# Expert gate and up products by Strassen's method, on two 128x64 column tiles

## The reference, cut to what matters

```python
def expert_choice_ffn(h, router, e_gate, e_up, e_down):
    ...
    cap = EC_FACTOR * t // N_EXPERTS
    ...
    gate, idx = lax.top_k(jnp.swapaxes(aff, 1, 2), cap)
    ...
    xe = h[bidx, idx]
    hid = jax.nn.silu(jnp.einsum('becd,edf->becf', xe, e_gate)) * jnp.einsum('becd,edf->becf', xe, e_up)
    ye = jnp.einsum('becf,efd->becd', hid, e_down) * gate[..., None].astype(h.dtype)
    return jnp.zeros_like(h).at[bidx, idx].add(ye)
```

## Time and profile before

| what | value |
|---|---|
| time, median of 3 runs | 3619.27 us (3618.79 to 3622.28) |
| span of the profiled execution | 3612.2 us |
| time of the runs outside the span (the difference of the two) | 7.1 us |
| TensorE matmul busy | 3408.1 us, 94% of the span |
| TensorE weight loads busy | 2976.7 us, 82% |
| VectorE busy | 1102.5 us, 31% |
| ScalarE busy | 735.5 us, 20% |

### The profile page before, as it was taken

The page is one execution under the profiler, slowest core; times in us unless marked ns, Lnnn a source line. Parts: engine busy times, 40 slices in busy tenths (PEclk is TensorE's granted clock), DMA queues, the critical chain, the costliest instruction groups (busy, mean ns, idle before and its releaser), DMA issues.

```text
span 3612.2 us, 83473 instructions
## 1 busy us (share of the span) xinstructions
PE 3408.1 (94%) x37698; PEld 2976.7 (82%) x37698; DVE 1102.5 (31%) x2770; ACT 735.5 (20%) x1815; POOL 385.0 (11%) x536
## 2 busy tenths in 40 slices
PE   7989898898999997499999999999999999999998
PEld 3575767667455544499999999999999999999998
DVE  4566666575344444411111111111111111111113
ACT  3435344343244433000000000000000000000002
POOL 0141514233211000000000000000000100000001
PEclk9999999999999998799999999999999999999999
DMA  8200000000311122697777778787778878777775
GB/s 353 71 5 9 18 10 17 5 20 5 102 32 26 43 77 93 226 362 264 281 269 275 268 274 275 264 288 258 272 276 280 275 267 283 263 281 269 274 264 185
DMA packets 500080, 666.46 MB, mean 185 GB/s; under 512 B 31598, under 2 KB 438406, under 8 KB 496654
## 3 DMA queue, kind: packets, MB, share of 16 engines
q1 hardware_dynamic: 494030, 641.74, 50.5%
q0 software_dynamic: 5520, 19.34, 2.0%
q10 hardware_dynamic: 176, 0.05, 0.0%
HBM read 631.68 MB, written 28.30 MB: 183 GB/s over the span
## 4 chain that ended last, share of the span: by engine, by line
PE 58%; SPq 1%; DMA 0%; DVE 0%; ACT 0%; issue 0%; DVEq 0%
PE banks L2465 38%; PE banks L2477 19%; PE banks L2488 0%; PE banks L2423 0%; DMA e_wd<-in_e_down 0%; SPq L2335 0%; SPq L2339 0%; SPq L2336 0%; SPq L2334 0%; ACT e_wd L2558 0%; PE banks L2447 0%; DVE e_ye L2632 0%; DVE e_wu L2718 0%; DVE e_wu L2661 0%; DVE e_xe L2707 0%
## 5 line engine op out<-in xcount | busy, mean ns | idle before, releaser
L2465 PE MATMUL banks<-e_xT,e_wg 128*128 128x144 f32 x5632 | 747.9, 287 | 1.9 <-DVE e_xT L2598 1.6
L2477 PE MATMUL banks<-e_hid,e_wd 128*128 128x144 f32 x5632 | 748.1, 287 | 0.0
L2465 PE MATMUL banks<-e_xT,e_wu 128*128 128x144 f32 x5632 | 747.6, 287 | 0.0
L2465 PEld LDWEIGHTS banks<-e_xT,e_wg 128*128 128x128 f32 x5632 | 713.8, 191 | 2.4 <-DMA e_wd<-in_e_down 2.3
L2465 PEld LDWEIGHTS banks<-e_xT,e_wu 128*128 128x128 f32 x5632 | 713.8, 191 | 0.0
L2477 PEld LDWEIGHTS banks<-e_hid,e_wd 128*128 128x128 f32 x5632 | 711.1, 191 | 0.0
L2608 DVE TENSOR_TENSOR e_tm<-banks,e_sg 128x144 f32<-128x144 f32 x352 | 108.3, 308 | 1790.3 <-ACT e_sg L2544 1790.3
L2544 ACT ACTIVATE e_sg<-banks 128x144 f32<-128x144 f32 x352 | 102.1, 290 | 1937.6 <-PE banks L2465 1937.6
L606 PE MATMUL banks<-hT_x,wblk 128*128 128x512 f32 (+1 forms) x624 | 212.7, 496 | 0.0
L606 PEld LDWEIGHTS banks<-hT_x,wblk 128*128 128x128 f32 x624 | 102.8, 192 | 100.1 <-issue 98.5
L1398 DVE TENSOR_TENSOR r_TW<-r_TW,banks 128x256 f32<-128x256 f32 (+1 forms) x360 | 129.3, 392 | 78.3 <-PE banks L830 74.1
(11 more groups left out here) (383 smaller groups left out, 3572.0 us busy)
## 6 DMA issues: line engine op xcount, KB each, us to landing
e_wg<-in_e_gate SPq DMA_DIRECT2D x176, 1024.0 KB, 5.2
e_wu<-in_e_up SPq DMA_DIRECT2D x176, 1024.0 KB, 7.5
e_wd<-in_e_down SPq DMA_DIRECT2D x176, 1024.0 KB, 10.2
h_wmod<-in_w_mod SPq DMA_DIRECT2D x24, 1024.0 KB, 15.2
wblk<-in_w_in SPq DMA_DIRECT2D x22, 512.0 KB, 21.5
h_x<-in_x_sample SPq DMA_DIRECT2D x8, 512.0 KB, 6.8
wo<-in_w_out SPq DMA_DIRECT2D x2, 2048.0 KB, 12.0
scratch_ffn<-hT_x SPq DMA_DIRECT2D x8, 512.0 KB, 5.2
```

The source lines that it names most:

```text
L2465: last = nc.tensor.matmul(bank[6 + b % 2][:, j * TOK:(j + 1) * TOK], w[s][:, k, f], xT[e % 2][:, k, :], start=(k == 0), stop=(k == KD - 1))
L2477: last = nc.tensor.matmul(bank[k // PER_BANK][:, c:c + TOK], wd[s][:, b % DUO, k * P:(k + 1) * P], hid[:, b % 2, :], start=(b == 0 and k % ...
```

## The change

Gate and up products of a duo are no longer made block by block as 8 pieces of 128 inputs each, but for the whole duo at once as a 2x2 block product: the weights of a duo are cut into halves by input (pieces 0 to 3 and 4 to 7) and by feature (block 0 and block 1), the tokens into halves by input and by token (72 and 72). Where a plain 2x2 block product takes eight half-size products, Strassen's method in Winograd's form takes seven, of which four use sums of blocks as an operand, and the four results are sums of the seven. So:

- VectorE forms three weight sums and one in place per duo, for gate and up together, 1024 elements per partition each (`sums_begin`, `sums_middle`, `sums_end`), two duos ahead, and four token sums per expert (`token_sums`).
- TensorE makes seven products for gate and seven for up, each over four pieces of 128 inputs, with 72 moving columns. The products of gate stand in bank 6 and those of up in bank 7. There is one set of banks, so gate and up of duo n+1 wait until those of n have been mixed (`gu_ok`).
- After them, ScalarE copies the first product out (`first`), and VectorE adds the results together in four steps (`mix`), then multiplies as before, for the whole duo at once (`gated`, `hidden`, 288 elements).
- Every matmul of the stage's main loop loads 128x64 weights and writes 64 PSUM partitions. Two neighbours write the two halves. The transposes of the loop become products with the identity matrix, in the same two halves (`turned`).
- Gate and up weights go into one buffer `wgu`, four deep, that is free when gate and up of the duo four earlier are done; down weights stay six deep. TensorE's order is gate and up of n+1, then the two halves of down of n, with transposes behind the halves in groups of four.

The diff, cut to its core:

```diff
-        wg = [sb(f"wg{i}", [P, KD, DUO * P]) for i in range(DEPTH)]
-        wu = [sb(f"wu{i}", [P, KD, DUO * P]) for i in range(DEPTH)]
-        wd = [sb(f"wd{i}", [P, DUO, D]) for i in range(DEPTH)]
+        wgu = [sb(f"wgu{i}", [P, 2, KD, DUO * P]) for i in range(WG)]
+        wd = [sb(f"wd{i}", [P, DUO, D]) for i in range(WD)]
+        wsum = [sb(f"wsum{i}", [P, 3, 2, HALF, P]) for i in range(2)]
...
+                    if n >= WG:
+                        sp.wait_ge(gu_ps, n - WG + 1)
+                    sp.dma_start(wgu[n % WG][:, 0, :, :], gv[:, e, :, f]).then_inc(g_in[n % WG], 16)
+                    sp.dma_start(wgu[n % WG][:, 1, :, :], uv[:, e, :, f]).then_inc(g_in[n % WG], 16)
+                    if n >= WD:
+                        sp.wait_ge(used, n - WD + 1)
...
+                def turned(b, out, src, n=P):
+
+                    for c in CS:
+                        if c.start < n:
+                            c = slice(c.start, min(c.stop, n))
+                            last = nc.tensor.matmul(bank[b][c, out], src[:, c], K.ident[:, :], start=True, stop=True)
+                    return last
...
+                def gate_up(n):
...
+                    pe.wait_ge(g_in[s], 32 * (n // WG + 1))
+                    pe.wait_ge(wsum_ok, n + 1)
+                    if n:
+                        pe.wait_ge(gu_ok, n)
...
+                    for g in range(2):
+                        w = wgu[s][:, g, :, :]
+                        products = ((w[:, k1, f1], x[:, k1, t1]), (w[:, k2, f1], x[:, k2, t1]),
+                                    (ws[:, 1, g, :, :], xs[:, 1, :, :]), (w[:, k1, f2], xs[:, 0, :, :]),
+                                    (ws[:, 0, g, :, :], x[:, k1, t2]), (ws[:, 2, g, :, :], x[:, k2, t2]),
+                                    (w[:, k2, f2], xs[:, 2, :, :]))
+                        for q, (a, b) in enumerate(products):
+                            for k in range(HALF):
+                                for c in CS:
+                                    last = nc.tensor.matmul(bank[6 + g][c, q * HT:(q + 1) * HT], a[:, k, c], b[:, k, :],
+                                                            start=(k == 0), stop=(k == HALF - 1))
+                    last.then_inc(gu_ps, 1)
...
+                gate_up(0)
+                for n in range(N):
+                    if n + 1 < N:
+                        gate_up(n + 1)
+                    down(n, 0)
+                    between(*divmod(n, ND), 0)
+                    down(n, 1)
+                    between(*divmod(n, ND), 1)
...
+                def sums_begin(n):
+
+                    a11, a12, a21, a22 = weight_blocks(n)
+                    dve.wait_ge(g_in[n % WG], 32 * (n // WG + 1))
+                    V.tensor_tensor(wsum[n % 2][:, 0, :, :, :], a11, a21, ALU.subtract).then_inc(ws_ok, 1)
+                    V.tensor_tensor(a21, a21, a22, ALU.add).then_inc(ws_ok, 1)
...
+                def mix(n):
...
+                    dve.wait_ge(gu_ps, n + 1)
+                    dve.wait_ge(first_ok, n + 1)
...
+                    V.tensor_tensor(gu[:, :, 0:4:3, :], first[:, :, :].unsqueeze(2).broadcast_to([P, 2, 2, HT]),
+                                    blocks(1, 2), ALU.add).then_inc(mix_ok, 1)
+                    dve.wait_ge(mix_ok, 2 * n + 1)
+                    V.tensor_tensor(mixed[:, :, :, :], gu[:, :, 3:4, :].broadcast_to([P, 2, 2, HT]), blocks(3, 2), ALU.add)\
+                     .then_inc(mix_ok, 1)
+                    dve.wait_ge(mix_ok, 2 * n + 2)
+                    V.tensor_tensor(gu[:, :, 1:3, :], mixed[:, :, :, :], blocks(5, 2), ALU.add)
+                    V.tensor_tensor(gu[:, :, 3:4, :], mixed[:, :, 1:2, :], blocks(3, 1), ALU.add).then_inc(gu_ok, 1)
...
+                for n in range(N):
+                    e, j = divmod(n, ND)
+                    mix(n)
+                    if n + 2 < N:
+                        sums_begin(n + 2)
+                    gated(n)
+                    if n + 2 < N:
+                        sums_middle(n + 2)
+                    hidden(n)
+                    if n + 2 < N:
+                        sums_end(n + 2)
```

319 lines of the change are left out of this document (167 added, 152 removed).

## The result

| | before | after |
|---|---|---|
| time, median | 3620.18 us (3618.79 to 3622.28, 4 runs) | 3724.38 us (3716.04 to 3726.98, 4 runs) |
| ratio, 95% interval | | 1.0289 (1.0275 to 1.0302) |
| span of the profiled execution | 3612.2 us | 3714.3 us |

The changed kernel is slower by 2.9% where the forecast had it faster by 2.9%. The page after, its lines that answer to the earlier trace rows: the span and the busy times, TensorE and VectorE in 40 slices, the transfers of instructions, the chain that ended last, and four groups of TensorE with their idle time and what ended it.

The account below looks back on a forecast made before the run. TensorE's instructions, one after another, were taken to bound the expert stage. Span 3612.2 - 148 (gate and up) + 30 (transposes) + 12 (start) + 3 (end) = 3509 us, plus 7.1 outside: 3516 us, range 3500 to 3570.

Parts of the forecast that it names:

- Gate and up, the slots: Gate and up products, expert stage: two halves run side by side, 112 slots of 62.5 ns, 7.00 us, 0.84 us less per duo.
- A: Rival on gate and up: slots last 64.4 ns or a little more, 37 us more, 3553 us; chance 0.17.
- B: Rival on gate and up: the two halves take turns, slots of 109 to 112 ns, about 4440 us; chance 0.06.
- Down and transposes: Expert stage: down stays at 122.5 ns a slot, 3.92 us per duo; transposes in two halves cost 30 us more.
- VectorE: VectorE's sums, mixing and multiplications in the expert stage: 7.5 of 10.92 us per duo, staying below TensorE.
- C: Rival: VectorE becomes the bound, needing sums of over 2.0 us; at 2.3 us a sum, 3715 us; chance 0.05.
- D: Rival: the new wait for `mix` shows; ending 0.3 us after down adds 53 us, 3569 us; chance 0.08.
- Start and end: Expert stage's ends: first transposes and sums delay the start by 12 us, late mixing in the last expert costs 3 us.
- Transfers: Weight transfers in the expert stage: 288 GB/s needed, four buffers instead of six, refills issued 22 us ahead; hidden.
- starts hold TensorE: Rival on TensorE's instruction starts: over 34 ns each the change would lose; the trace shows 14.4 ns; chance 0.01.
- T1b: Experiments' theory, not the prediction's: instruction pieces wait while weight transfers run; without those, about 3550 us or less expected.
- T1a: Experiments' theory, not the prediction's: instruction pieces come late by their own latency; without weight transfers, 3700 to 3725 us expected.

## Why the prediction was wrong

**What bounds the kernel.** Right for the kernel before. "So the stage costs what TensorE's instructions cost one after another" is what did not carry over: it holds as long as the instructions are there.

**Gate and up, the slots.** Right: 62.5 ns, so A (64.4 ns) and B (halves in turns) did not happen. The choice of the line through the long forms was right too: 72, 96 and 144 columns lie on one line of 0.83 ns a column through 62.5, 82.4 and 122.0 ns. That line would give 56 ns at 64 columns, a little less than the 58 ns of the four-tile row. That this row is bound by its weight loads, the reason given, was not tested.

**Down and transposes.** Right: 3.9 us, and 30 us against 31.8 measured with tiles alone.

**VectorE.** Right in its parts: the sums took 1.22 us, 1.14 apart, the mix 0.45, 0.45, 0.45 and 0.30:

```profile
2508.33 0.45 DVE L2687 TENSOR_TENSOR e_gu<-e_first,banks 128x288 f32<-128x288 f32 x1 [4.92 <-PE banks L2495]
2508.82 0.45 DVE L2690 TENSOR_TENSOR e_mixed<-e_gu,banks 128x288 f32<-128x288 f32 x1
2509.30 0.45 DVE L2693 TENSOR_TENSOR e_gu<-e_mixed,banks 128x288 f32<-128x288 f32 x1
2509.68 0.30 DVE L2694 TENSOR_TENSOR e_gu<-e_mixed,banks 128x144 f32<-128x144 f32 x1
```

`mix` ends at 2509.98, and the next gate and up products start at 2512.43, behind down and some transposes: hidden, as forecast. C and D did not happen. The sign "VectorE at 65 to 70% in the stage" was missed (57.78 of 100 us), as a duo took longer; without weight transfers it is 66.08.

**Start and end.** Right: 12 us and 3 us were forecast. Products began at 1503.91 against 1494.90, with 2.22 us between duo 0 and 1, and down of the last duo waited for 1.77 us:

```profile
1503.91 2.19 PE L2495 MATMUL banks<-e_xT,e_wgu 128*64 128x72 f32 x32 [8.21 <-DVE e_wsum L2670]
...
1515.53 1.22 PE L2495 MATMUL banks<-e_xT,e_wgu 128*64 128x72 f32 x32 [2.22 <-DVE e_gu L2694]
...
3692.04 4.14 PE L2510 MATMUL banks<-e_hid,e_wd 128*64 128x144 f32 x64 [1.77 <-DVE e_hid L2702]
```

**Transfers.** "Hidden" was asked for the weights alone, and for them it is true: the chain has DMA at 0%. That they delay another queue, the one that brings TensorE's instructions, was put at nothing without being asked. This is the step that failed, and with it "Gate and up: 112 x 62.5 = 7.00 us", which holds only while instructions are there: over the stage a slot took 72.6 ns (twice the 36.3 below), above the 67.7 ns from which the prediction itself has the change lose. The rival that came nearest, "starts hold TensorE", failed with them. That one had the right border, a mean of 34 ns a start from which the change loses: gate and up took 1415.5 us for 38,977 passes, 36.3 ns each. It had the wrong mechanism, and was dismissed by 98 passes at 14.4 ns: 98 passes are fewer than the 128 of one piece, so they say how fast TensorE starts what it has, not how fast it is fed. The prediction also weighed the 25 and 62 ns a start that the Trainium skill gives ("TensorE: Matmul & The Clock Gate", Wait — 56ns, not 53.3ns?); both are too long for the 14.4 ns, and neither made the loss. None of the three cases that "Wrong if" names came about (slots above 64.5 ns, but for the stops; a wait for `mix`; sums of over 2 us): the prediction did not look for the one that did.

The sum of the forecast was right but for this: without weight transfers the kernel takes 3521.69 us, 0.9736 of before, and the forecast was 3516 us, 0.9715. One term was read wrongly without harm: the 7.1 us "outside the span" are mostly the difference between two executions, as executions of the same kernel on record with both figures have 1.7 to 1.8 us (3716.04 against 3714.3). The missing 203 us (3724.38 - 3521.69; 200 by the ratios) are TensorE's stops: over the whole stage, from 1520 us on, they are 190 us by the measure of the table's last column (174 in gate and up, 16 in down), and the gate and up passes between them took 31.9 ns in place of 31.5, 14 us more, shorter stops among them. The page's own numbers were there to ask: instructions went from 83,473 to 153,923, the added ones all in a stage where the earlier trace rows have the DMA engines busy for 0.75. In the page of the kernel before, two rows carry the mark of it, the count of the pieces and a group that waits for "issue":

```profile
q8 instruction: 297, 4.87, 0.5%
...
L823 PE MATMUL banks<-r_X,r_TW 64*64 64x64 f32 x2304 | 111.1, 229 | 7.2 <-issue 4.2
```

and its timeline, in the mixer stage with its short 64x64 passes, where no semaphore stands in front:

```profile
607.12 0.27 PE L852 MATMUL banks<-r_S,r_QR 64*64 64x64 f32 x2 [0.84 <-issue]
611.07 0.28 PE L771 MATMUL banks<-r_vtok,r_M 64*64 64x64 f32 x3 [0.76 <-issue]
```

These two restarts are 127 matmuls apart, and each comes 2.4 us after a packet of q8 started (604.71 and 608.63): the same stop, in the kernel before. And it comes there without any burst of transfers, as the DMA share in the stretch shows (0.04, the last number but one):

```profile
600.00:800.00 200.00, 178.96 (x4371) 135.41 (x4365) 128.64 (x298) 86.00 (x218) 67.09 (x102) 1.00 0.04 12
```

The pieces in it start 3.8 us apart (median), so the stream has a rate of its own too, by this about one piece in 3.8 us or 30 ns a matmul. The changed kernel's 31 ns just keep to it, with next to nothing left to catch up in after a delay; that is the part of T1a in the loss, while the delays themselves are T1b.

The Trainium skill says in "Runtime: NRT & Kernel Launch", Instruction fetch mechanics, that an engine fetches its instructions through a DMA queue of its own in blocks of 16 KiB or 256 instructions, and that the cost of crossing such a block is "mostly hidden". The distance of the stops bears out the first; the second does not hold here, once 256 instructions last 4 us beside bursts of weight transfers.

**What stays open.** Why a late piece inside a burst starts 3 us into it in one case and 11 us in another, the runs do not tell; nor do they tell which part of the 2.2 to 2.5 us from a transfer's start to the restart is more than the 0.96 us that its packet took. That the weight transfers delay the pieces is shown; in what way is not. How much stands queued on the DMA engines at one time would fit the four kernels that differ in size and spacing of their transfers, but this is argued from them, not seen in the DMA engines' own order of work.

## What to carry to other kernels

A change that makes TensorE's instructions shorter and more numerous has to be costed by the stream that feeds them too: 128 matmuls with their weight loads come as one piece, and it must last long enough for the next to arrive. Pieces came some 3.8 us apart where nothing else was transferred, and less evenly beside weights: with weights issued in bursts, pieces that lasted 4.0 us left 174 us of stops, and pieces of 5.3 us (96 columns, 128 x 41.2 ns) left 3.3. Count the instructions per us before and after, look for "issue" in the chain and among the groups, and check whether idle moments stand 128 matmuls apart. If they do, spread the large transfers over the time of the work, by waits on steps of TensorE, rather than issuing them together when a buffer falls free; here that turned a loss of 2.9% into a gain of 1.2 to 1.5%.

## What the hardware showed unexpectedly

- The transfer of a piece of instructions (16.4 KB, 0.96 us a packet) starts late beside bursts of weight transfers: of the 182 late ones, 133 began 3 to 11 us into a burst and 48 at its end. TensorE restarts 2.2 to 2.5 us after it begins.
- Without any weight transfers, pieces started hardly ever less than 3.8 us apart (5th percentile), just below the 4.0 us that 128 passes of 72 columns last. In the mixer stage, with its 64x64 passes and the DMA engines nearly idle (0.04), TensorE stopped at the ends of pieces too.
- Float32 passes on 128x64 column tiles, two side by side, cost 62.5, 82.4 and 122.0 ns a pair for 72, 96 and 144 columns.
- A change from two column tiles to the whole array cost 0.10 us, the change back 0.20 us.
